# Loading the second expert batch's down weights in halves

## The reference

```
mix = hybrid_mixer(x, w_in[l], ..., w_out[l])       # three kinds of attention, 16 heads, one output projection
x   = layer_norm(ALPHA * x + mix, ln1_g[l], ln1_b[l])
ffn = moe_ffn(x, router_w, router_b, w1[l], w3[l], w2[l])
x   = layer_norm(ALPHA * x + ffn, ln2_g[l], ln2_b[l])
# moe_ffn: each token goes to 2 of 64 experts; an expert is (silu(x @ w1) * (x @ w3)) @ w2
#          w1, w3: 1024 x 256, w2: 256 x 1024, so 3 MB of weights for an expert, 192 MB for a layer
```

## Time and profile before

| what | us |
|---|---|
| median of 3 runs | 1151.63 |
| lowest and highest of them | 1149.08, 1152.26 |
| the profiled execution's own time | 1153.33 |
| its span, first to last instruction | 1151.6 |
| TensorE busy | 1048.4 (91%) |
| VectorE, ScalarE busy | 406.0 (35%), 271.3 (24%) |
| queue q1 | 439.52 MB, 93.1% of 16 DMA engines |

### The profile page before, as it was taken

One profiled execution on the slowest core, in us unless ns is written; L12 is line 12 of the kernel. 1 busy time (PEld: TensorE's weight loads), 2 busy tenths in 40 slices (PEclk: granted clock), 3 DMA queues, 4 the chain that ended last, 5 costly groups with the idle time before them and its releaser, 6 DMA issues.

```text
span 1151.6 us, 28954 instructions
## 1 busy us (share of the span) xinstructions
PE 1048.4 (91%) x12450; PEld 537.3 (47%) x12450; DVE 406.0 (35%) x1207; ACT 271.3 (24%) x714; POOL 18.8 (2%) x36
## 2 busy tenths in 40 slices
PE   9999999998998998888899999988989989988887
PEld 6665664443444443333456657434444444434333
DVE  4875352222222222122268656322222222222213
ACT  1244241111212111111132544211121111111111
POOL 0010000000000000000000100000000000000000
PEclk9999999999999999999999999999999999999999
DMA  9958599999999999999995687999999999999996
GB/s 302 326 219 328 194 407 425 427 428 429 428 429 429 429 428 430 429 428 429 390 322 183 262 310 294 409 426 426 428 428 429 429 429 429 429 429 430 428 429 233
DMA packets 69103, 440.81 MB, mean 383 GB/s; under 512 B 16065, under 2 KB 35649, under 8 KB 43201
## 3 DMA queue, kind: packets, MB, share of 16 engines
q1 hardware_dynamic: 68768, 439.52, 93.1%
q0 software_dynamic: 144, 0.58, 0.1%
q10 hardware_dynamic: 144, 0.07, 0.0%
HBM read 439.10 MB, written 1.05 MB: 382 GB/s over the span
## 4 chain that ended last, share of the span: by engine, by line
PE 88%; DVE 7%; issue 3%; DMA 1%; SPq 1%; ACT 0%; POOL 0%; DVEq 0%
PE bank L1078 19%; PE bank L1167 17%; PE bank L1057 10%; PE bank L1179 10%; PE bank L691 8%; PE bank L817 4%; PE bank L1130 3%; DVE moe L1681 2%; DVE moe L1739 2%; PE bank L1173 1%; PE bank L961 1%; PE bank L1153 1%; DMA w_even<-in_w_in 1%; DVE moe L1698 1%; PE bank L680 1%
## 5 line engine op out<-in xcount | busy, mean ns | idle before, releaser
L1812 ACT ACTIVATE moe<-bank 128x512 f32<-128x512 f32 (+2 forms) x164 | 84.0, 524 | 556.4 <-PE bank L1078 331.3
L1681 DVE COPY moe<-bank 128x512 f32<-128x512 f32 (+1 forms) x66 | 44.6, 676 | 323.4 <-PE bank L1078 311.3
L1179 PE MATMUL bank<-moe 128*128 128x512 f32 (+1 forms) x264 | 119.5, 593 | 26.0 <-DVE moe L1739 22.5
L1057 PE MATMUL bank<-moe,x 128*64 128x64 f32 x3840 | 122.1, 224 | 0.9 <-issue 0.9
L1057 PEld LDWEIGHTS bank<-moe,x 128*64 128x64 f32 x3840 | 117.8, 138 | 6.0 <-issue 6.0
L1078 PE MATMUL bank<-w_even,moe 64*32 64x512 f32 x1792 | 107.0, 624 | 12.5 <-issue 12.5
L1078 PE MATMUL bank<-w_odd,moe 64*32 64x512 f32 x1920 | 107.5, 591 | 3.7 <-issue 3.7
L1167 PE MATMUL bank<-w_even,moe 64*32 64x512 f32 x896 | 99.0, 590 | 10.1 <-DVE moe L1698 10.1
L1167 PE MATMUL bank<-w_odd,moe 64*32 64x512 f32 x896 | 99.0, 590 | 9.3 <-DVE moe L1698 9.3
L1972 ACT ACTIVATE moe<-bank,small 128x64 f32<-128x64 f32 x240 | 74.4, 416 | 106.9 <-PE bank L1057 106.9
L1179 PEld LDWEIGHTS bank<-moe 128*128 128x128 f32 x264 | 47.2, 189 | 100.3 <-DVE moe L1739 47.9
(11 more groups left out here) (200 smaller groups left out, 891.5 us busy)
## 6 DMA issues: line engine op xcount, KB each, us to landing
w_odd<-in_moe_w SPq DMA_DIRECT2D x92, 2048.0 KB, 30.9
w_even<-in_moe_w SPq DMA_DIRECT2D x82, 2048.0 KB, 33.4
w_even<-in_moe_w SPq DMA_DIRECT2D x28, 1024.0 KB, 8.8
w_even<-in_w_in SPq DMA_DIRECT2D x24, 768.0 KB, 11.1
w_odd<-in_w_out SPq DMA_DIRECT2D x4, 2048.0 KB, 15.0
w_odd<-in_moe_w SPq DMA_DIRECT2D x4, 1024.0 KB, 44.5
w_odd<-in_moe_w SPq DMA_DIRECT2D x8, 512.0 KB, 13.6
w_even<-in_w_in SPq DMA_DIRECT2D x4, 416.0 KB, 7.4
```

The costliest lines, as they stand in the source:

```text
L1057: last = mm(bank[2 + h][64 * z:64 * z + 64, 64 * c:64 * c + 64], xc_pair[:, t, h, c, :], chosen_pair[:, t, z], start=t == 0, stop=t == 1)
L1179: return mm(Y[t][h][:, lo - 512 * h:hi - 512 * h], scatter[:, t * P:(t + 1) * P], y_rows[:, lo:hi], start=False, stop=True, skip_group_che ...
L1681: return nc.vector.tensor_copy(partial[:, k, cols], source[:, cols])
L1812: return fn(dst, src, ACT.Copy)
```

## The change

The loader takes a slice of a pair's four steps, and both down pairs of batch 1 are loaded as two loads of 1 MB in place of one of 2 MB. The later halves (steps 2 and 3) move up in SyncE's order: pair 1's goes behind a new wait for `upT_psum` 2, after the loads of experts 0 and 1 and ahead of the wait for `comb` 8, and pair 0's goes ahead of the wait for `z_psum` 2. The earlier halves stay where the whole pairs were. The semaphore's count in `down_pairs` follows.

```diff
-                def load_w2_pair(e, q, parity):
-                    sp.dma_start(w2_pairs[parity][q].rearrange("p c d -> p (c d)"),
-                                 w2_pair[l * (NE // 2) + e * (NB // 2) + q]).then_inc(w2_in[parity][2 * q].sem, 16)
+                def load_w2_pair(e, q, parity, steps=slice(0, 4)):
+                    cols = slice(steps.start * DM, steps.stop * DM)
+                    sp.dma_start(w2_pairs[parity][q][:, steps, :].rearrange("p c d -> p (c d)"),
+                                 w2_pair[l * (NE // 2) + e * (NB // 2) + q][:, cols]).then_inc(w2_in[parity][2 * q].sem, 16)
...
                 load_w13(0)
                 load_w13(1)
+                after(sp, l, upT_psum, 2)
+                load_w2_pair(1, 1, 1, slice(2, 4))
                 after(sp, l, comb, 8)
...
                 after(sp, l, ropT_psum, 8)
-                load_w2_pair(1, 1, 1)
+                load_w2_pair(1, 1, 1, slice(0, 2))
...
                 load_w13_pair(1, 0, 0, 1)
+                load_w2_pair(1, 0, 1, slice(2, 4))
                 after(sp, l, z_psum, 2)
-                load_w2_pair(1, 0, 1)
+                load_w2_pair(1, 0, 1, slice(0, 2))
...
-                        pe.wait_ge(w2_in[parity][k].sem, (b0 + j) * 8 + (8 - 16 * l if parity else 16))
+                        pe.wait_ge(w2_in[parity][k].sem, (b0 + j) * 8 + (24 if parity else 16))
```

## The result

| what | before | with the change |
|---|---|---|
| median, us | 1151.38 (1149.08 to 1152.26, 6 runs) | 1145.51 (1145.11 to 1146.27, 6 runs) |
| ratio to before | | 0.9949, 95% interval 0.9938 to 0.9961 |
| the profiled execution, its span | 1153.33, 1151.6 | 1145.58, 1143.8 |

The change makes the kernel 5.9 us faster, 0.5%. Timed a second time beside before it was 1145.44 against 1151.45, ratio 0.9947 (0.9933 to 0.9961).

The account below looks back on a forecast made before the run. The expert stage was taken as bound by DMA, its stream starting from TensorE's attention stage. Layer 0's 4.3 us (2.6 + 1.7) and layer 1's 1.43, together 5.7, off 1151.63 gave 1145.9 us, range 1143.8 to 1149.5.

Parts of the forecast that it names:

- The bound and the path: Expert stage is DMA-bound, its stream starts from TensorE's events; each microsecond saved in the attention stage reaches the layer's end.
- The shift of the landing: Second output half, behind 1 MB in place of 2, lands 2.6 us earlier (bounds 2.4 and 2.7) in each layer.
- sign of 11 to 12: Sign that the forecast holds: the second output half lands 11 to 12 us after its issue.
- The two waits: TensorE's idle time before out_chunk(0, 1, 0): 2.84 us in layer 0, 2.6 of it gained; 1.43 in layer 1, all gained.
- The clock's term: Layer 0, six products after the idle stretch: clock stays whole once the stretch is short, gaining 1.70 us.
- Rival 1: Waits go, but most timed runs lack the clock's share, or 2.84 shrinks partly: 1147.6 to 1148.3 us; chance 0.13.
- The profiled execution's own gain: Whole kernel, one profiled execution: 1153.33 - 4.3 - 1.43 = 1147.6 us.
- The early half, the late half, the wait for `upT_psum` 2: Pair 1's half landing by about 60.6 in the idle queue, pair 0's later half, and the new wait: zero each.
- Rival 2: Expert stage: its stream does not start from TensorE's events, so the gain is hidden, about 1151 us; chance 0.08.
- rival 3: Expert stage's stream: each load pays its start in line, +2.0 us a layer, 1149.9 us; chance 0.07.
- rival 4: Half pairs move at a lower rate; gain used up at 3.6 us a half, 1161 at 4.9; chance 0.06 with rival 5.
- Rival 5: SyncE's order: if `comb` 8 ended before `upT_psum` 2, the new wait would hold later loads; chance 0.06 with rival 4.

Follow-up runs that it names:

- the 14 matmuls: The changed kernel with 14 matmuls of 128x128 (28 instructions) added ahead of out_chunk(0, 1, 0) in each layer: 1152.02 us, 1.0014 against before.
- pair 1 alone: The changed kernel with pair 0 put back to one load, so only pair 1's down load is halved: 1145.49 us, ratio 0.9952.
- all pairs halved: The changed kernel with every later down pair (batches 2 to 14, both layers) also loaded as two halves, 52 loads more: 1150.25 us.
- Pair 0 alone: The changed kernel with pair 1 put back to one load, so only pair 0's down load is halved: 1151.53 against 1151.63 us, ratio 1.0006.

## Why the prediction was right

**The bound and the path** held. The gain arises at the two waits for the second output half, and the expert stages keep their length (to 0.1 us in this pair, within about 1 us over all traces) and start earlier. That time of TensorE before them counts in full was argued from rows 2 and 12; the 28 added instructions a layer showed it, to about 1 us in 6.3.

**The shift of the landing** (2.6 us): in layer 1 it is right but for one trace, 12.7 to 13.0 before and 10.0 to 10.3 in five of the six traces with 1 MB ahead; the one with the 14 matmuls has 11.7. In layer 0 it was mis-sized: the six with 1 MB ahead (the changed kernel and its two repetitions, pair 1 alone, the 14 matmuls, all pairs halved) have 10.0, 11.7, 10.2, 11.5, 10.2 and 10.4, four with 2 MB have 14.1 to 14.4, a shift of 2.4 to 4.4. The prediction's sign of 11 to 12 fits only two of the six. The shift in layer 0 is never smaller than the bytes account for; what adds up to 1.8 there is open. It changed little, as 2.6 leaves only 0.2 to 0.4 us of the wait.

**The two waits** were worth a little more than their idle time. Before, layer 0's stretch was 28.04 - 23.27 = 4.77, made of 2.84 idle, 1.70 clock and 0.23 for the pipeline's new start; layer 1's was 24.94 - 23.27 = 1.67, made of 1.43 and 0.24. The prediction left those 0.2 out, and in layer 0 also the last 0.25 of the idle time, which it expected to stay: 6.44 in place of 5.7.

**The clock's term** (1.70) is what was only half right, and it makes the closeness of the forecast (1145.9, measured 1145.51) in part luck. It was read from one execution as part of every one. It is there in two of the four profiled executions in which TensorE waited 2.84 to 3.10 us. With it the waits are worth 6.4, without it 4.7; the medians give 5.9. A term taken whole and terms left out came near to cancelling. Rival 1 named the chance; how many of the timed executions lost the 1.70 is not shown, so neither is how far rival 1 holds.

**The profiled execution's own gain** was put at 5.7 and was 7.75. The last store's landing makes 1.7 of the difference, the terms left out above, less small differences elsewhere, the rest. The median was the better thing to predict.

**The early half, the late half, the wait for `upT_psum` 2:** zero, as predicted. The early half landed at 60.8 (60.6 forecast). No wait for VectorE or ScalarE came up on TensorE between 107 and 134. Pair 0 alone is no gain and no loss, so half of the change does nothing.

**Rival 2** falls by the 14 matmuls, **rival 3** by the 52 loads, apart from its remnant of 0.07 to 0.09 us a load, **rival 4** by the same run: a half that took 3.6 us in place of 2.45, its break-even, would have cost 104 x 1.15 = 120 us there, and 4.7 were seen. **Rival 5** falls by the early issue (53.77) and landing (60.8) and by the issues behind it, which start at 64.85 (64.64 before, in an execution that is 0.2 ahead at TensorE's products too).

## What to carry to other kernels

When an engine waits for a load, look first at what was issued ahead of it in the same queue and when that is needed: here 2 MB that are read 90 us later stood ahead of 2 MB that are read at once, and an exchange of two lines gives as much as loading by halves. In a program whose later stage is bound by transfers, time saved ahead of the stage's first dependent transfer counts in full. That time saved inside the stage counts nothing was not tested, but rows point to it: in the expert stage, products that took 3.67 us in place of 5.37 were followed by a wait of 3.06 in place of 1.38 (the second repetition of before at 1065.52, the first execution at 1037.48). And one profile is one execution: a term that may come and go (a lowered clock, the last store) belongs in the sum with its share, not whole.

## What the runs showed of the hardware

- The granted clock after TensorE had been idle ahead of `out_chunk(0, 1, 0)`: 1.00 after 1.43 and 1.59 us (and up to 1.75); lowered in two cases of four after 2.84 to 3.10 (0.68 and 0.69 in the window behind; 2.93 lowered, 3.10 not); lowered after 3.83 and 5.22 (0.66). 0.66 to 0.69 over 5 us is a mixture of the full 2.4 GHz and 1.2 GHz, and it cost 1.7 to 2.6 us of the six products. In the expert stage it is as uncertain: the four stretches of 3.07 to 3.17 us in the first execution of before were each followed by products in 5.30 to 5.37 us, and of the four of 3.06 to 3.19 in its second repetition one was not (3.67 us after 3.06).
- A load of 1 MB more in a full queue, its bytes being moved anyway, costs 0.07 to 0.09 us. Alone, a load of 1 MB lands in 4.7 us and one of 2 MB in 7.4, so 2.0 us of it do not grow with the bytes.
- The last store of 256 KB landed 2.5 us after its issue in some executions and 4.2 in others of the same kernel.
